# Seven-product pairs every third pair, their weight sums made a pair ahead, two of them by accumulating DMA transfers, and the banks of the two output halves swapped

## The reference

```python
def sq_relu_mlp(h, w1, w2):
    return jnp.square(jax.nn.relu(h @ w1)) @ w2
...
        x = x + g1 * y
        h2 = modulate(rmsnorm(x, norm2_g[l]), sh2, sc2)
        x = x + g2 * sq_relu_mlp(h2, w1[l], w2[l])
    return rmsnorm(x, final_norm_g)
```

## Time and profile before

| | |
|---|---|
| median of 3 runs | 1503.91 us |
| the profiled execution | 1502.44 us, span 1500.6 us |
| TensorE busy | 1462.5 us, 97% of the span |
| VectorE busy | 1099.9 us, 73% |
| ScalarE busy | 707.2 us, 47% |
| POOL busy | 117.3 us, 8% |
| from HBM | 352.60 MB, 236 GB/s over the span |

### The profile page before, as it was taken

How to read it: one execution, slowest core, us unless ns; L and a number is a source line. 1 busy time by engine, 2 the same in 40 slices (tenths; PEclk the granted TensorE clock), 3 DMA queues, 4 the chain that set the end, 5 groups by cost and what they waited for, 6 DMA issues and landing times.

```text
span 1500.6 us, 18815 instructions
## 1 busy us (share of the span) xinstructions
PE 1462.5 (97%) x7255; PEld 1201.4 (80%) x7255; DVE 1099.9 (73%) x1334; ACT 707.2 (47%) x992; POOL 117.3 (8%) x88
## 2 busy tenths in 40 slices
PE   5999999999999999999999999999999999999997
PEld 2567888888888888888888888888887888878885
DVE  2456866867666678988677577877657888799886
ACT  3433444565445453344454443443444665456544
POOL 0000000101000000010100000001101232023100
PEclk9999999999999999999999999999999999999999
DMA  9997776755767679889755578778665666656662
GB/s 368 377 360 254 263 259 207 226 187 165 232 206 242 205 230 367 332 290 356 236 197 168 181 235 305 270 269 297 193 192 175 189 203 199 199 180 200 198 197 78
DMA packets 123053, 355.95 MB, mean 237 GB/s; under 512 B 10962, under 2 KB 11986, under 8 KB 122322
## 3 DMA queue, kind: packets, MB, share of 16 engines
q1 hardware_dynamic: 121348, 353.17, 69.8%
q10 hardware_dynamic: 1616, 1.57, 0.3%
HBM read 352.60 MB, written 2.10 MB: 236 GB/s over the span
## 4 chain that ended last, share of the span: by engine, by line
PE 84%; DVE 9%; DMA 2%; ACT 2%; issue 2%; POOL 0%; ACTq 0%; POOLq 0%; DVEq 0%
PE bank L1673 19%; PE bank L1675 19%; PE bank L1674 19%; PE bank L1959 14%; PE bank L1962 7%; DVE wl L1193 2%; PE bank L1829 2%; PE bank L1802 1%; DMA raw<-in_w_ada 1%; ACT wh L738 1%; PE bank L1704 1%; PE bank L1792 1%; DVE acc L1224 1%; DMA ident<-in_identity 1%; DVE tL L1569 0%
## 5 line engine op out<-in xcount | busy, mean ns | idle before, releaser
L1193 DVE TENSOR_TENSOR wl<-raw,wh 128x1024 fp32r<-128x1024 f32 x427 | 522.7, 1243 | 220.5 <-ACT wh L738 208.6
L738 ACT ACTIVATE wh<-raw 128x1024 fp32r<-128x1024 f32 x328 | 341.6, 1059 | 295.4 <-PE bank L1962 141.3
L1959 PE MATMUL bank<-h2S,wh 128*128 128x512 f32 x896 | 244.9, 394 | 0.8 <-DVE wl L1193 0.7
L1673 PE MATMUL bank<-wh,hT 128*128 128x512 f32 x512 | 206.7, 404 | 0.6 <-DVE wl L1193 0.6
L1675 PE MATMUL bank<-wh,hT 128*128 128x512 f32 x512 | 200.1, 391 | 0.0
L1674 PE MATMUL bank<-wl,hT 128*128 128x512 f32 x512 | 199.7, 390 | 0.0
L1959 PEld LDWEIGHTS bank<-h2S,wh 128*128 128x128 f32 x896 | 153.2, 189 | 21.6 <-DVE wl L1193 0.9
L1673 PE MATMUL bank<-wh,hidS 128*128 128x512 f32 x400 | 155.8, 389 | 1.0 <-issue 0.7
L1675 PE MATMUL bank<-wh,hidS 128*128 128x512 f32 x400 | 155.6, 389 | 0.0
L1674 PE MATMUL bank<-wl,hidS 128*128 128x512 f32 x400 | 155.6, 389 | 0.0
L1224 DVE SCALAR_TENSOR_TENSOR acc<-raw,cc,acc 128x1024 f32<-128x1024 f32 x120 | 153.5, 1279 | 0.0
(11 more groups left out here) (254 smaller groups left out, 2060.3 us busy)
## 6 DMA issues: line engine op xcount, KB each, us to landing
raw<-in_w SPq DMA_DIRECT2D x256, 512.0 KB, 4.7
raw<-in_w_ada SPq DMA_DIRECT2D x192, 512.0 KB, 5.8
raw<-in_w_in SPq DMA_DIRECT2D x128, 512.0 KB, 4.6
raw<-in_w_attn_o SPq DMA_DIRECT2D x32, 512.0 KB, 6.5
raw<-in_w_out SPq DMA_DIRECT2D x32, 512.0 KB, 6.3
raw<-in_w_fourier SPq DMA_DIRECT2D x16, 512.0 KB, 6.5
xt<-in_x SPq DMA_DIRECT2D x2, 1024.0 KB, 6.2
ct<-in_ctx SPq DMA_DIRECT2D x2, 1024.0 KB, 10.8
```

Of the source, the lines that this page charges most:

```text
L738: nc.scalar.activation(slot, raw[:, s % RAW, :], ACT.Copy).then_inc(wh_done, 1)
L1193: nc.vector.tensor_tensor(lo, raw[:, s % RAW, :], hi.bitcast(F32), ALU.subtract)\
L1673: nc.tensor.matmul(bank[b][:], a_hi, w_hi, start=first, stop=False)
L1959: nc.tensor.matmul(out[:], wh[:, slot, cols_f[f]], h2S[:, block, :, :].rearrange("p v t -> p (v t)"), start=(block == 0), stop=False)
```

## The change

- Seven-product pairs stand at every third pair: 8 in the first half (3 to 24), 7 in the second (5 to 23), so 15 instead of 14.
- Two of the four weight sums are no longer made by VectorE. `tS`, two buffers of two 128x512 blocks, is filled twice by a plain load of r1's right block on SP's queue, and then POOL issues two accumulating transfers, which add r1's left block to the one copy and r2's right block to the other.
- The two other sums (`block_sums`) are made by VectorE at the end of the pair before. `tL` stands first in the seven-product pair, and `tH` ahead of `wh`.
- TensorE waits for both tL before the first of the seven products.
- The second half sums its plain parts in banks 4 to 7 and its other terms in 0 to 3. Pair 32 waits for `combined`, pair 37 for `z_free`. Reading the first half's parts moves to pairs 34 and 35.
- `combine` has its first two steps in one pair, in a region `comb` of its own; `prescaled` is spread over pairs 38, 41, 44 and 47; four squares move to pairs 38 to 41; at the end the mean of the first token half stands ahead of `gated(6)`, and the square of part 6 ahead of the first scalings.

```diff
@@ -221,17 +221,20 @@
-SEVEN_AT = ((2, 5, 9, 12, 16, 19, 23), (0, 3, 7, 10, 14, 17, 21))
+SEVEN_AT = ((3, 6, 9, 12, 15, 18, 21, 24), (5, 8, 11, 14, 17, 20, 23))
+SEVENS_TO = (len(SEVEN_AT[0]), len(SEVEN_AT[0]) + len(SEVEN_AT[1]))
...
-COMBINE_AT = {2: "first", 3: "second", 4: 0, 5: 1, 6: 2, 7: 3}
+COMBINE_AT = {3: ("first", "second"), 4: (0,), 5: (1,), 6: (2,), 7: (3,)}
+TAKEN_AT = {2: (0, 1), 3: (2, 3)}
+PRESCALED_AT = {6: 0, 9: 1, 12: 2, 15: 3}
...
         tL = place("tL", [P, 4, HC], F32R, "h", 16384)
         scr2 = place("scr2", [P, 4, HC], F32, "h", 24576)
+        comb = place("comb", [P, 4, HC], F32, "h", 16384)
+        tS = [place("tS0", [P, 2, HC], F32, "h"), place("tS1", [P, 2, HC], F32, "f", 4096)]
         aF = place("aF", [P, 4, P], F32, "f")
         junk_2 = place("junk_2", [P, HC], F32, "f", 2048)
...
+        def plain_bank(c, b):
+            return 4 * c + b
+
+        def seven_bank(c, b):
+            return 4 * (1 - c) + b
+
...
                 sp.dma_start(raw[:, (S2 + n) % RAW, :], w2[k * P:(k + 1) * P, col * NC:(col + 1) * NC]).then_inc(raw_full[(S2 + n) % RAW], 16)
+                i, e = divmod(n - RAW + 7, 2)
+                if e == 0 and i in SEVENS:
+                    s = SEVENS.index(i)
+                    c, p = divmod(i, NP)
+                    if s == 0:
+                        sp.wait_ge(gemm_done, M2)
+                    if s >= 2:
+                        sp.wait_ge(t_lo, 2 * s - 2)
+                        sp.wait_ge(t_sum, s - 1)
+                    for j in range(2):
+                        sp.dma_start(tS[s % 2][:, j, :], w2[2 * p * P:(2 * p + 1) * P, c * NC + HC:(c + 1) * NC]).then_inc(t_first[s % 2], 16)
...
+                pool.wait_ge(t_first[s % 2], 32 * (s // 2 + 1))
+                row, col = 2 * p * P, i // NP * NC
+                nc.gpsimd.dma_start(tS[s % 2][:, 0, :], w2[row:row + P, col:col + HC], accum_op=ALU.add).then_inc(t_acc[s % 2], 16)
+                nc.gpsimd.dma_start(tS[s % 2][:, 1, :], w2[row + P:row + 2 * P, col + HC:col + NC], accum_op=ALU.add).then_inc(t_acc[s % 2], 16)
                 if s:
                     pool.wait_ge(a_lo, 3 * s)
                 then(nc.gpsimd.tensor_tensor(aF[:, 0, :], hid[:, k2, P:T], hid[:, k1, P:T], ALU.subtract))
...
                 nc.scalar.activation(aH[:, 6, :], hid[:, 2 * p + 1, P:T], ACT.Copy).then_inc(a_hi, 1)
                 act.wait_ge(a_sum, s + 1)
                 nc.scalar.activation(aH[:, 0:4, :], aF[:], ACT.Copy).then_inc(a_hi, 1)
+                act.wait_ge(t_acc[s % 2], 32 * (s // 2 + 1))
+                nc.scalar.activation(tH[:, 0:2, :], tS[s % 2][:], ACT.Copy).then_inc(t_hi, 1)
+                act.wait_ge(t_sum, s + 1)
+                nc.scalar.activation(tH[:, 2:4, :], tF[:], ACT.Copy).then_inc(t_hi, 1)
                 tile_hi(2 * i, HC)
                 tile_hi(2 * i + 1)
-                for j in range(2):
-                    act.wait_ge(wl_done, W2 + 2 * i + j + 1)
-                    nc.scalar.activation(tH[:, 2 * j:2 * j + 2, :], tF[:, 2 * j:2 * j + 2, :], ACT.Copy).then_inc(t_hi, 1)
...
-                if ps == 1 and 3 <= p < 7:
-                    last_square(p - 3)
+                if ps == 1 and 6 <= p < 10:
+                    last_square(p - 6)
...
             last_square(5)
+            last_square(6)
             act.wait_ge(rs2_ready, 1)
             last_scaled(0, 4)
             last_scaled(2, 4)
-            last_square(6)
             last_square(7)
...
+                following = PAIRS[i + 1][2] if i + 1 < len(PAIRS) else None
+                for e in range(2):
+                    n = 2 * i + e
                     split_lo(W2 + n + 1, S2 + n, wh[:, n % SPL, :], wl[:, n % SPL, :])
+                if following is not None:
+                    block_sums(i + 1, following)
+
+            def block_sums(i, s):
+                n2 = 2 * i + 1
+                r2 = raw[:, (S2 + n2) % RAW, :]
+                dve.wait_ge(raw_full[(S2 + n2) % RAW], 16 * ((S2 + n2) // RAW + 1))
+                dve.wait_ge(t_acc[s % 2], 32 * (s // 2 + 1))
+                if s:
+                    dve.wait_ge(t_hi, 2 * s)
+                then(nc.vector.tensor_tensor(tF[:, 0, :], tS[s % 2][:, 0, :], r2[:, HC:NC], ALU.add))
+                nc.vector.tensor_tensor(tF[:, 1, :], tF[:, 0, :], r2[:, 0:HC], ALU.add).then_inc(t_sum, 1)
 
             def seven_lo(i, p, s):
                 n1, n2 = 2 * i, 2 * i + 1
-                r1, r2 = raw[:, (S2 + n1) % RAW, :], raw[:, (S2 + n2) % RAW, :]
+                for j in range(2):
+                    dve.wait_ge(t_hi, 2 * s + j + 1)
+                    if j:
+                        dve.wait_ge(t_sum, s + 1)
+                    part = slice(2 * j, 2 * j + 2)
+                    nc.vector.tensor_tensor(tL[:, part, :], (tS[s % 2], tF)[j][:], tH[:, part, :].bitcast(F32), ALU.subtract).then_inc(t_lo, 1)
                 dve.wait_ge(a_hi, 3 * s + 2)
                 for part, src in ((slice(4, 6), hid[:, 2 * p:2 * p + 2, 0:P]), (slice(6, 7), hid[:, 2 * p + 1:2 * p + 2, P:T])):
                     nc.vector.tensor_tensor(aL[:, part, :], src, aH[:, part, :].bitcast(F32), ALU.subtract).then_inc(a_lo, 1)
                 dve.wait_ge(a_hi, 3 * s + 3)
                 nc.vector.tensor_tensor(aL[:, 0:4, :], aF[:], aH[:, 0:4, :].bitcast(F32), ALU.subtract).then_inc(a_lo, 1)
-                dve.wait_ge(wh_done, W2 + n1 + 1)
-                nc.vector.tensor_tensor(wl[:, n1 % SPL, 0:HC], r1[:, 0:HC], wh[:, n1 % SPL, 0:HC].bitcast(F32), ALU.subtract)
-                if s:
-                    dve.wait_ge(t_hi, 2 * s)
-                nc.vector.tensor_tensor(tF[:, 0, :], r1[:, 0:HC], r1[:, HC:NC], ALU.add)
-                dve.wait_ge(raw_full[(S2 + n2) % RAW], 16 * ((S2 + n2) // RAW + 1))
-                nc.vector.tensor_tensor(tF[:, 1, :], r1[:, HC:NC], r2[:, HC:NC], ALU.add).then_inc(wl_done, 1)
-                dve.wait_ge(wh_done, W2 + n2 + 1)
-                nc.vector.tensor_tensor(wl[:, n2 % SPL, :], r2, wh[:, n2 % SPL, :].bitcast(F32), ALU.subtract)
-                dve.wait_ge(wl_done, W2 + n1 + 1)
-                then(nc.vector.tensor_tensor(tF[:, 2, :], tF[:, 0, :], r2[:, HC:NC], ALU.add))
-                nc.vector.tensor_tensor(tF[:, 3, :], tF[:, 2, :], r2[:, 0:HC], ALU.add).then_inc(wl_done, 1)
-                dve.wait_ge(wl_done, W2 + n2 + 1)
-                for j in range(2):
-                    dve.wait_ge(t_hi, 2 * s + j + 1)
-                    part = slice(2 * j, 2 * j + 2)
-                    nc.vector.tensor_tensor(tL[:, part, :], tF[:, part, :], tH[:, part, :].bitcast(F32), ALU.subtract).then_inc(t_lo, 1)
+                for n, width in ((n1, HC), (n2, NC)):
+                    dve.wait_ge(wh_done, W2 + n + 1)
+                    nc.vector.tensor_tensor(wl[:, n % SPL, 0:width], raw[:, (S2 + n) % RAW, 0:width],
+                                            wh[:, n % SPL, 0:width].bitcast(F32), ALU.subtract).then_inc(wl_done, 1)
...
-                    dve.wait_ge(gemm_done, M2 + 2 * NP)
-                    for n in range(4):
+                for step in COMBINE_AT.get(p - SEVEN_AT[ps][-1], ()):
+                    combine(ps, step)
+                if ps == 1:
+                    if p == 2:
+                        dve.wait_ge(gemm_done, M2 + 2 * NP)
+                    for n in TAKEN_AT.get(p, ()):
                         taken(n)
-                if ps == 1 and p == 1:
-                    for n in range(4):
+                    for n in TAKEN_AT.get(p, ()):
                         added(n)
-                if ps == 1 and p == 9:
-                    dve.wait_ge(fg_in, 16)
-                    dve.wait_ge(x2_ready, 4)
-                if ps == 1 and 9 <= p < 13:
-                    prescaled(p - 9)
+                    if p in PRESCALED_AT:
+                        dve.wait_ge(fg_in, 16)
+                        dve.wait_ge(x2_ready, 4)
+                        prescaled(PRESCALED_AT[p])
 
             gated(4)
             gated(5)
+            last_mean(0)
             gated(6)
-            last_mean(0)
...
-                    if i == NP + 1 and e == 0:
-                        pe.wait_ge(z_free, 4)
+                    if i == NP and e == 0:
+                        pe.wait_ge(combined, 1)
                     for b in range(4):
                         half, t = divmod(b, 2)
-                        first = e == 0 and (i == 0 or (i == NP + 1 and b == 3))
                         w, cols_t = slice(half * HC, (half + 1) * HC), slice(t * P, (t + 1) * P)
-                        ins = products(b, [(hidS[0][:, x % 2, e, cols_t], hidS[1][:, x % 2, e, cols_t],
-                                            wh[:, n % SPL, w], wl[:, n % SPL, w])], first, n == 2 * NP - 1)
+                        ins = products(plain_bank(c, b), [(hidS[0][:, x % 2, e, cols_t], hidS[1][:, x % 2, e, cols_t],
+                                                           wh[:, n % SPL, w], wl[:, n % SPL, w])],
```

(49 more changed lines are left out.)

33 lines of the change are left out of this document (14 added, 19 removed).

## The result

The change makes the kernel slower: 1513.91 us median (1512.47 to 1514.63, 4 runs) against 1503.88 for the kernel before in the same comparison; ratio 1.0065, 95% interval 1.0047 to 1.0082. The prediction said 1495.0, with a range of 1491 to 1506. The profiled execution took 1512.47 us, with a span of 1510.7.

A forecast was written before the change was run, and what follows sets the result against it. TensorE, busy 97% of the span, was taken as the bound. Terms -0.7 - 4.1 - 4.4 + 1.0 - 0.5 = -8.7 took the profiled 1502.44 us to 1493.7, stated as a median of 1495.0, range 1491 to 1506.

The forecast's parts named there:

- Part 1: Last product: fifteen seven-product pairs in place of 14 mean 3 matmuls fewer, -0.7 us.
- Part 2: VectorE: two of four sums leave it, a seven-product pair falls from 9.1 to 7.5 us, sparing 2 us a period.
- part 3: Seven-product pairs: sums made a pair ahead and tL first end the waits at 1269 and 1395; 0.3 us is left.
- Parts 3 and 4: Last product: sums a pair ahead and swapped banks remove waits at the half and long intervals, saving 4.1 of 4.45 us.
- Part 5: First seven-product pair, coming one pair later: loss falls from 5.8 to 1.4 us with no slow clock, -4.4.
- Part 6: Added plain and accumulating transfers: they fit by 1.3 us and 2.8 more before TensorE feels it; +1.0 for stray waits.
- Slower from a chain of about 11 us on: Threshold in rival A: at 0.6 us a pair the gain is gone, so such a transfer chain makes the kernel slower.
- Part 7: Combining at pair 27, prescaling every third pair, squares at pairs 38 to 41: same operations in plain pairs, costing nothing.
- Part 8: Tail after the last product: the sixth square ahead of the scalings starts earlier, -0.5 us.
- A: Rival: issues and landings of the accumulating transfers make seven-product pairs late; slower, middle 1512 us, chance 0.18.
- B: Rival: at the first seven-product pair POOL's first transfer or aF costs several us, clock fallen; 4.4 given back, 1499.4, chance 0.13.
- C: Rival: small waits of 0.5 us at each of 15 pairs, no change overall, 1502.5 us, chance 0.09.

The follow-up runs named there:

- e4: The changed kernel without the added transfers, VectorE making all four sums at the end of the pair before; 1491.55 us median.
- e12: e8 with both halves using the same banks, leaving new pair places, steps placed after them and new end; within its expected 1493.5 to 1494.3 us.
- e9: The changed kernel plus a fill and tiny sum on GpSimd in idle time before the last product, no added transfer; first pair loses 7.9 us instead of 14.5.
- e10: e7 with two semaphores each for loads and accumulating transfers, used in turn; 18 us come back, still loses 14 us more than e4.
- e6: The changed kernel with e1's early transfer and sum plus e3's earlier plain loads; beats the kernel before the change by 4.4 us.
- e2: The changed kernel with GpSimd's aF sums ahead of its two transfers for the first seven-product pair alone; that pair loses 12.4 us instead of 14.5.
- e7: e4 and e1 together, all 60 transfers running into an unread tile, one semaphore for loads and one for accumulating transfers; 1525.4 us.
- e8: e4 with the order inside a seven-product pair put back to that before the change; went as its rival said, 1491.5 to 1493 us.
- e11: e4 with both halves using the same banks instead of swapped ones; 1.8 us slower than e4 by the medians.
- e1: The changed kernel plus one tiny accumulating transfer and one tiny sum on GpSimd in idle time before the last product; came out as expected, median 1508.
- e5: The changed kernel with GpSimd's two transfers as plain copies, leaving out two weight sums; 2.2 us below the expected 1507 to 1509.
- e3: The changed kernel with SP issuing the plain loads one pair earlier from the third seven-product pair on; 1505.5 us.

## Why the prediction was wrong

By its own parts:

- **Part 1** (three matmuls fewer): right, 7252 for 7255.
- **Part 2** (VectorE's relief): right in size, 15 us less, and worth nothing, as e4 shows with all four sums on VectorE. The prediction took the relief as a condition of part 3 without asking if the old load would have fitted as well: by its own prices it is 2 x 3.1 + 9.1 = 15.3 of 15.7 us a period.
- **Parts 3 and 4** (-4.1 of 4.45): the stalls at 1269, 1318 to 1337 and 1395 are gone, so the sum is right. Its attribution is not: e12 keeps 2.1 of the 4.5 with neither sums ahead nor swapped banks, so the even spacing of the pairs, with the steps placed after them, gives over half; banks give 1.6, sums ahead the rest.
- **Part 5** (first pair 5.8 to 1.4) is the step that failed most: 14.5, so 13.1 us of the 18.8 by which the sum missed the profiled time (1493.7 against 1512.47). Two of its terms broke. The first is "POOL's aF, queued behind the issues, takes 4.9, to 1152.9": it ended at 1163.4. The prediction charged the moved step for its own issues, but not for being the first thing on GpSimd after the all-reduce, where a cost of 7.6 to 11 us had lain in 88 us of idle time. e9 moves it back, aF ends at 1153.4, and 6.6 of the 13.1 go. The second is "landed at 1151.5", and it makes the other 6.5: in e9 the transfers landed at 1158.2. 2.9 us of that are a wait that the prediction left out: it let GpSimd issue at 1145.64, but the plain loads, which SP issues only at 1141.2 or later, must land first, and they did at 1147.5 in the changed kernel and 1147.9 in e9. The other 3.8 are the landing: 9.7 from the first issue until both had landed, instead of 5.9.

  The prediction's "I charge no slow clock" failed with them: gaps of 3.3 (before), 4.5 (e10), 5.9 (e6) and 11.7 us are followed by steps of 0.43 us, half the clock. The length of the gap alone does not tell when this happens: one of 2.4 us (e2) is followed by full-speed steps, and e7 has gaps of 2.5 and 2.2 us with a few full-speed steps behind them and then some eight at half the clock. The gap of 2.2, and a row from among the slow steps behind it:

```profile
1445.73 0.47 PE L1717 MATMUL bank<-wh,aH 128*128 128x512 f32 x1 [2.17 <-DVE wl L1613]
...
1447.77 0.63 PE L1718 MATMUL bank<-tL,aH 128*128 128x512 f32 x1
```

- **Part 6** (transfers, +1.0 for stray waits): the issues at 0.9 and 1.2 us were right. The landing was mis-sized: 2.4 + 3.5 = 5.9 us were put from the first issue until both transfers had landed, and the changed kernel has 10.1 in the median (6.2 to 11.7). The plain loads, 7.2 in the median until both had landed (5.4 to 8.9), were slower too than the 6.5 that the bandwidth sum gave, though that counts from the raw tile ahead of them. The value of 3.5 was chosen by the store of 256 KB, the nearest row in size; the nearest in kind was the raw tile, 4.8, beside busy queues. The DMA share was near the forecast, 0.71 of the stretch where 0.8 stood. Six later pairs lose 6.7 us in all, where 1.3 stood for all pairs with the 0.3 of part 3: 5.4 too little. "Slower from a chain of about 11 us on" did not decide: from the second load's landing until both transfers had landed it took 10.4 us in the median (7.1 to 12.0), and those 5.4 us alone would have left 3.3 of the forecast gain of 8.7. It is with the first pair that the kernel became slower.
- **Part 7**: no wait of its own in any trace. **Part 8** (-0.5): the last reduction of the squares starts 2.64 after the last product instead of 3.13, the last issue 5.50 instead of 5.99: right. Yet the span ends 4.35 after that instead of 3.78, and 4.3 to 4.5 after it in six of the experiments; in the other six (e4, e7, e8, e10, e11, e12) it ends as before. What tells them apart stays open.

Of the rivals, A (slower, middle 1512) names the outcome and nearly its time, and its mechanism, the accumulating landing, is at work in both places: 5.4 us over the forecast between the pairs, and the greater part of the 6.5 in the first pair. B's mechanism ("the first POOL transfer costs several us more, or aF behind it does ... with the clock fallen") is the other 6.6, half as much again as its price of 4.4. They had been priced one at a time, as alternatives, and came together; that A's middle lies 2 us from the result is luck, since it stood for 15 late pairs and no gap on GpSimd. C (small waits at each pair, VectorE too tight) did not happen: in e4 VectorE lets TensorE wait twice, 0.3 us each.

The gain forecast for the rest of the change was a little too small. Without part 6 the sum gives -9.7; e4, which is the change without the transfers, is 12.3 us faster by the medians and 11.1 by the profiled spans. Its 1491.55 is the lower end of the forecast's own range, 1491.5, "no stray waits and a first pair on time". The transfers took 22.4 us back.

## What to carry to other kernels

Before work is moved to another engine, show that the first engine lacks the time for it: here it had it, and the move cost 22 us (and still 8 with both remedies, e6 against e4). When the first instruction of a long idle engine is moved or replaced, ask what ran unseen in that idle time (here GpSimd's way back from an all-reduce); one small instruction of the right kind in the idle time puts it back. Give a two-stage transfer the lead of two whole landings, measured beside traffic, and count what stands behind it in the same queue as waiting with it. When two late things end in one wait, remove both before judging either: here each alone hid the other.

## What the runs showed of the hardware

- GpSimd's first ordinary instruction after a partition all-reduce starts 7.6 us late (e9), 9.8 (e1), 11.2 (changed kernel) or 11.4 (e5), after MODIFY_POOL_CONFIG; a fill (0.17 us at 1057.00 in e9) and DMA issues before it are not held.
- An accumulating transfer of 256 KB from GpSimd's queue: issue 0.9 to 1.2 us, landing 8.3 (median, changed kernel) or 6.8 (e3, issued a pair earlier); plain 5.8 (e5). For the same bytes it takes 1.8 times the packets of the plain one, 2 KB each instead of 4, and 1.76 times the engines' time.
- With all loads on one semaphore and all accumulating transfers on another, GpSimd's second issue was held 5.5 to 8.0 us in six of 15 pairs (e7); with two of each in turn never (e10).
- Behind gaps of 3.3 to 11.7 us at the first seven-product pair TensorE's steps last 0.43 us instead of 0.227 for a while, at half the clock; behind gaps of 2.2 and 2.5 us in e7 too, but not behind one of 2.4 in e2.
